# Head 7 of a two-layer trunk built from seven products for eight, like heads 2 to 6 before it

## What is computed

```python
h = rmsnorm(x, g_pre_mix)
z = h @ w_in                     # 1024 -> B | C | xin | c_q | c_kv | k_rope | gate_conv | gate_mla
yc, new_buf = short_conv(c_g * xin, conv_buf, conv_w)    # three causal taps
y_a = b_g * yc
y_b = mla_attention(q_nope, q_pe, pos, ckv_all, kpe_all, k_pos, w_uk, w_uv)    # 8 heads
merged = sigmoid(gate_conv) * y_a + sigmoid(gate_mla) * y_b
x = x + rmsnorm(merged @ w_o, g_post_mix)
x = x + rmsnorm(square(relu(rmsnorm(x, g_pre_ffn) @ w1)) @ w2, g_post_ffn)
```

## Time and profile before

| | |
|---|---|
| time of the profiled execution | 1719.35 us |
| its span in the profile | 1717.5 us |
| granted TensorE clock, mean | 0.998 |
| TensorE busy | 1704.5 us, 99%, 12735 matmuls |
| VectorE busy | 1313.3 us, 76% |
| ScalarE busy | 862.5 us, 50% |
| POOL busy | 122.3 us, 7% |
| chain that ended last | 95% TensorE, 3% VectorE, 1% DMA, 1% issue |
| weight blocks of 512 KB, issue to landing | 3.7 us median of 197 |
| sums of weights, made by POOL's DMAs | 80 of 256 KB: 7.1 us; 20 of 512 KB: 5.4; 40 of 256 KB from sums: 7.6 (medians) |

### The profile page before, as it was taken

How to read it: one execution, slowest core, us unless ns; L and a number is a source line. 1 busy time by engine, 2 the same in 40 slices (tenths; PEclk the granted TensorE clock), 3 DMA queues, 4 the chain that set the end, 5 groups by cost and what they waited for, 6 DMA issues and landing times.

```text
span 1717.5 us, 31904 instructions
## 1 busy us (share of the span) xinstructions
PE 1704.5 (99%) x12735; PEld 1690.0 (98%) x12735; DVE 1313.3 (76%) x2512; ACT 862.5 (50%) x1669; POOL 122.3 (7%) x163
## 2 busy tenths in 40 slices
PE   9999999999999999999999999999999999999997
PEld 9999999999999999999999999999999999999997
DVE  7788877767798777668688788777678887777665
ACT  7636454544554544446366364545446636444452
POOL 1412222122200000000000000000000000000000
PEclk9999999999999999999999999999999999999999
DMA  7888989898842323233133234443433313322231
GB/s 240 199 191 181 230 207 216 188 265 214 175 110 63 111 82 92 87 98 99 62 119 123 90 116 128 116 127 114 162 118 99 99 39 110 99 87 87 74 99 56
DMA packets 85619, 222.09 MB, mean 129 GB/s; under 512 B 9568, under 2 KB 21088, under 8 KB 85472
## 3 DMA queue, kind: packets, MB, share of 16 engines
q1 hardware_dynamic: 66592, 176.01, 32.1%
q0 software_dynamic: 17600, 41.95, 13.8%
q10 hardware_dynamic: 1280, 2.10, 0.4%
HBM read 209.67 MB, written 52.30 MB: 153 GB/s over the span
## 4 chain that ended last, share of the span: by engine, by line
PE 95%; DVE 3%; DMA 1%; issue 1%; ACT 0%; SPq 0%; DVEq 0%; ACTq 0%
PE ring L817 19%; PE ring L819 19%; PE ring L818 19%; PE att L817 11%; PE att L819 11%; PE att L818 11%; DMA w_raw<-blocks_in 1%; PE att L3589 1%; DVE w_lo L2092 1%; PE att L812 1%; PE att L811 1%; PE att L824 0%; PE att L3405 0%; PE att L825 0%; PE att L3744 0%
## 5 line engine op out<-in xcount | busy, mean ns | idle before, releaser
L817 PE MATMUL ring<-xs_hi,w_lo 128*128 128x288 f32 x1872 | 556.5, 297 | 1.2 <-DVE w_lo L2092 0.5
L819 PE MATMUL ring<-xs_hi,w_hi 128*128 128x288 f32 x1872 | 551.5, 295 | 0.0
L818 PE MATMUL ring<-xs_lo,w_hi 128*128 128x288 f32 x1872 | 551.3, 294 | 0.0
L2092 DVE TENSOR_TENSOR w_lo<-w_raw,w_hi 128x1024 fp32r<-128x1024 f32 (+1 forms) x364 | 370.8, 1038 | 38.7 <-ACT w_hi L1209 28.6
L817 PEld LDWEIGHTS ring<-xs_hi,w_lo 128*128 128x128 f32 x1872 | 351.6, 188 | 3.9 <-DVE w_lo L2092 1.3
L818 PEld LDWEIGHTS ring<-xs_lo,w_hi 128*128 128x128 f32 x1872 | 351.8, 188 | 1.4
L819 PEld LDWEIGHTS ring<-xs_hi,w_hi 128*128 128x128 f32 x1872 | 351.6, 188 | 0.0
L819 PE MATMUL att<-f_hi,w_hi 128*128 128x288 f32 x960 | 283.2, 295 | 0.0
L818 PE MATMUL att<-f_lo,w_hi 128*128 128x288 f32 x960 | 282.9, 295 | 0.0
L817 PE MATMUL att<-f_hi,w_lo 128*128 128x288 f32 x960 | 282.6, 294 | 0.0
L817 PEld LDWEIGHTS att<-f_hi,w_lo 128*128 128x128 f32 x960 | 180.4, 188 | 0.0
(11 more groups left out here) (346 smaller groups left out, 3189.9 us busy)
## 6 DMA issues: line engine op xcount, KB each, us to landing
w_raw<-blocks_in SPq DMA_DIRECT2D x197, 512.0 KB, 3.7
weight_sums<-blocks_in POOLq DMA_DIRECT2D x80, 256.0 KB, 7.1
w_raw<-blocks_in SPq DMA_DIRECT2D x58, 256.0 KB, 4.1
weight_sums<-blocks_in POOLq DMA_DIRECT2D x20, 512.0 KB, 5.4
weight_sums<-weight_sums POOLq DMA_DIRECT2D x40, 256.0 KB, 7.6
w_raw<-weight_sums SPq DMA_DIRECT2D x20, 512.0 KB, 4.6
w_raw<-weight_sums SPq DMA_DIRECT2D x40, 256.0 KB, 4.2
small_raw<-small_in SPq DMA_DIRECT2D x16, 320.0 KB, 4.0
```

The source lines that it names most:

```text
L817: pe.matmul(out, w[1], x[0], start=first, stop=False)
L818: pe.matmul(out, w[0], x[1], start=False, stop=False)
L819: return pe.matmul(out, w[0], x[0], start=False, stop=last)
L2092: return dve.tensor_tensor(out, a, hi.bitcast(F32), ALU.subtract)
```

## The change

- `LAST_MIXED` goes from 6 to 7: head 7 is a mixed head. There are 24 sums of weights in place of 20 (two couples per mixed head and layer), three more positions, and the extra slot takes turns with the others up to position eight (`N_EXTRA` 8).
- Head 7 has an order of its own (`MIXED_ORDER`): TensorE does product (0,0) to (0,3), projections, (0,4) to (0,6), scores, (1,0) to (1,3), turns, (1,4), (1,5), attended, block B (both halves), (1,6). The other mixed heads do block B ahead of the turns.
- VectorE: `last_mixed_head`, written out below. `small_lo(8)` moves from head 7 to behind the second `wo_out_a`, that is behind the first sample scaling; ScalarE's `small_hi(8)` to behind `wo_hi(5)`. The cache splits 0 and 1 move to behind the first four row splits. Gates with rx are plain multiplications in plain heads now (only 0 and 1 are left).
- ScalarE: rows 0 to 3 are split, then the weights of w_o 2 and 3, the copies of the new cache rows, rows 4 to 6, the second gate, row 7.
- SP: rows 0 and 1 of my are reloaded at j = 4, rows 2 to 5 (two parts) at j = 5, row 6 at j = 6, with a semaphore for rows 0 to 3 and another for the rest; cache_t and cache_pe are loaded behind the projections of head 7, cache_n and the small weights 8 at j = 6.
- Row 0 of my is kept from another place (`my[:, 5]`), and the four turned inputs lie in another order in the space of `my`.

The diff, cut (lines of context are left out):

```diff
@@ -82,7 +82,7 @@
...
-FIRST_MIXED, LAST_MIXED = 2, 6
+FIRST_MIXED, LAST_MIXED = 2, HEADS - 1
...
@@ -91,7 +91,7 @@
-N_EXTRA = 5
+N_EXTRA = 8
...
@@ -132,8 +132,8 @@
...
-        two = any(is_mixed(h) and HEAD_POS[h] + (3 if h == FIRST_MIXED else 2) <= q < HEAD_POS[h] + 7
-                  for h in range(HEADS))
+        two = any(is_mixed(h) and HEAD_POS[h] + (3 if h == FIRST_MIXED else 2) <= q
+                  < HEAD_POS[h] + (8 if h == LAST_MIXED else 7) for h in range(HEADS))
...
@@ -173,7 +173,7 @@
...
-    return pl.my[:, KC - 1, :] if k in (0, HEADS - 1) else pl.rx2[:, :]
+    return pl.my[:, 5, :] if k == 0 else pl.my[:, KC - 1, :] if k == HEADS - 1 else pl.rx2[:, :]
...
@@ -222,16 +222,17 @@
...
-FIRST_ORDER = [0, 1, 7, 8, 2, 3, 4, 5, 6]
+MIXED_ORDER = {FIRST_MIXED: [0, 1, 7, 8, 2, 3, 4, 5, 6, 9, 10, 11, 12, 13, 14, 15],
+               LAST_MIXED: [0, 1, 2, 3, 4, 5, 6, 9, 10, 11, 12, 13, 14, 7, 8, 15]}
+
+
+def mixed_part(h, n):
+
+    return MIXED_ORDER[h].index(n) if h in MIXED_ORDER else n
...
-    return HD0 + HEAD_BANKS[h] + (FIRST_ORDER.index(i) if h == FIRST_MIXED and i < 9 else i)
-
-
-def mixed_part(h, n):
-
-    return FIRST_ORDER.index(n) if h == FIRST_MIXED and n < 9 else n
+    return HD0 + HEAD_BANKS[h] + mixed_part(h, i)
...
@@ -949,12 +955,13 @@
...
-                if j in (begun, 5):
-                    sp.wait_ge(pl.sums_third, 16 * (head_sums(L, h, j // 5) + 1))
+                second = 4 if h == LAST_MIXED else 5
+                if j in (begun, second):
+                    sp.wait_ge(pl.sums_third, 16 * (head_sums(L, h, j // second) + 1))
...
-                if j in (begun, 7):
+                if j == begun or j == 7 and h != LAST_MIXED:
...
@@ -984,28 +991,34 @@
...
-                if h == HEADS - 1:
-                    sp.wait_ge(pl.my_stored, stored(L, HEADS - 2))
...
-                    if j == (4 if h == FIRST_MIXED else 3 if is_mixed(h) else 2):
+                    if h < LAST_MIXED and j == (4 if h == FIRST_MIXED else 3 if is_mixed(h) else 2):
...
-                    if h == HEADS - 1 and j == 2:
+                    if h == LAST_MIXED and j == 2:
+                        sp.wait_ge(pl.projected, L * 40 + 39)
...
-                        sp.wait_ge(pl.scored, (L + 1) * HEADS * KT)
-                        sp.dma_start(pl.naraw[:, :, :], cache_n[L]).then_inc(pl.nat_landed, 16)
...
-                        last = (1, 8, 3, 5, 9, 11, 13, 15) if h == FIRST_MIXED else (1, 3, 5, 8, 9, 11, 13, 15)
+                        last = (1, 8, 3, 5, 9, 11, 13, 15) if h == FIRST_MIXED else \
+                            (1, 3, 5, 9, 11, 13, 8, 15) if h == LAST_MIXED else (1, 3, 5, 8, 9, 11, 13, 15)
+                        if h == LAST_MIXED and j == 6:
+                            sp.wait_ge(pl.ring_full, full(L, r_mixed(h, 14)))
+                            my_load(3)
+                            sp.dma_start(pl.naraw[:, :, :], cache_n[L]).then_inc(pl.nat_landed, 16)
+                            next_small(h)
...
-                    if h == HEADS - 1:
-                        for n in ((0, 1), (2,), (3,), (), ())[j]:
-                            my_load(n)
+                    if h == LAST_MIXED and j == 4:
+                        sp.wait_ge(pl.my_stored, stored(L, HEADS - 2))
+                        my_load(0)
+                    if h == LAST_MIXED and j == 5:
+                        my_load(1)
+                        my_load(2)
...
@@ -1504,9 +1517,6 @@
...
-                if h == HEADS - 1:
-                    next_weight(-2)
-                    next_weight(-1)
...
@@ -1618,6 +1620,11 @@
...
+
+                def last_gates():
+                    eng.wait_ge(pl.ring_free, freed(L, r_mixed(h, 14)))
+                    act.activation(pl.ga[:, :], pl.ga[:, :], ACT.Tanh, scale=0.5)
+                    act.activation(pl.gb[:, cols(0)], pl.gb[:, cols(0)], ACT.Tanh, scale=0.5).then_inc(pl.gated, 1)
...
@@ -1645,6 +1652,26 @@
...
+                if h == LAST_MIXED:
+                    snapshot(0)
+                    pos_hi(L, at + 2)
+                    query_hi(h)
+                    pos_hi(L, at + 3)
+                    keys_hi(h)
+                    pos_hi(L, at + 4)
+                    pos_hi(L, at + 5)
+                    absorbed_hi(h)
+                    conv_started()
+                    snapshot(1)
+                    exponents(h)
+                    pos_hi(L, at + 6)
+                    turned_hi(h)
+                    pos_hi(L, at + 7)
+                    caches_hi()
+                    pos_hi(L, at + 8)
+                    last_gates()
+                    pos_hi(L, at + 9)
+                    return
...
@@ -1673,16 +1700,33 @@
...
-                if k < HEADS - 1:
-                    eng.wait_ge(pl.my_landed, 64 * (L + 1))
+                if k < 4:
+                    eng.wait_ge(pl.my_landed, 32 * (L + 1))
+                elif k < HEADS - 1:
+                    eng.wait_ge(pl.my_landed_rest, 32 * (L + 1))
...
-            eng.wait_ge(pl.ring_full, full(L, r_hd(HEADS - 1, 4, 0)))
-            for k in range(HEADS):
+            eng.wait_ge(pl.ring_full, full(L, r_mixed(LAST_MIXED, 7)))
+            for k in range(4):
...
+            pos_hi(L, POSITIONS + 2)
+            pos_hi(L, POSITIONS + 3)
+            eng.wait_ge(pl.latent_lo, L * 4 + 4)
+            eng.wait_ge(pl.key_lo, L * 2 + 2)
+            apart()
+            for to, src in ((pl.cth, pl.kvh), (pl.ctl, pl.kvl)):
+                act.activation(to[:, :, PAST:NT], src[:, :, NP_:NT].bitcast(F32), ACT.Copy)
+            for to, src in ((pl.kch, pl.keh), (pl.kcl, pl.kel)):
+                ins = act.activation(to[:, PAST:NT], src[:, NP_:NT].bitcast(F32), ACT.Copy)
+            ins.then_inc(pl.cache_new, 1)
+            for k in range(4, HEADS - 1):
+                x_hi_a(k)
+            eng.wait_ge(pl.ring_free, freed(L, r_mixed(LAST_MIXED, 15)))
+            act.activation(pl.gb[:, cols(1)], pl.gb[:, cols(1)], ACT.Tanh, scale=0.5).then_inc(pl.gated, 1)
+            x_hi_a(HEADS - 1)
...
@@ -1729,6 +1773,7 @@
...
+            small_hi(L, HEADS)
...
@@ -2586,20 +2629,16 @@
...
-                if h == HEADS - 1:
-                    cache_lo(1, pl.kcl[:, 0:PAST], pl.kcraw[:, 0:PAST], pl.kch[:, 0:PAST])
...
-                if h < FIRST_MIXED:
-                    own.wait()
-                    own.step(dve.tensor_tensor(pl.ga[:, :], pl.ga[:, :], pl.rx[:, :], ALU.mult))
-                if h != FIRST_MIXED - 1:
+                own.wait()
+                own.step(dve.tensor_tensor(pl.ga[:, :], pl.ga[:, :], pl.rx[:, :], ALU.mult))
+                if first:
...
-                if h < FIRST_MIXED - 1:
...
@@ -2774,8 +2812,76 @@
...
+                def last_mixed_head():
+                    upper_left(0, pl.cv[:, cols(0)])
+                    first_difference(0)
+                    second_sum(0)
+                    pos_lo(L, at + 2)
+                    query_lo(h, 0)
+                    query_lo(h, 1)
+                    pos_lo(L, at + 3)
+                    keys_lo(h)
+                    conv_state(h)
+                    lower_left(0, pl.u[:, 2:2 + NH])
+                    conv_first_half()
+                    lower_right(0, pl.v2[:, :])
+                    upper_right(0, pl.cv[:, cols(1)])
+                    conv_second_half()
+                    pos_lo(L, at + 4)
+                    pos_lo(L, at + 5)
+                    row_maxima(h)
+                    absorbed_lo(h, pl.rest)
+                    upper_left(1, pl.gb[:, cols(0)])
+                    conv_taps(h)
+                    first_difference(1)
+                    probabilities(h)
+                    second_sum(1)
+                    pos_lo(L, at + 6)
+                    turned_lo(h)
+                    lower_left(1, pl.ga[:, cols(0)])
+                    pos_lo(L, at + 7)
+                    lower_right(1, pl.ga[:, cols(1)])
+                    pos_lo(L, at + 8)
+                    src = ready(7)
+                    dve.tensor_tensor(pl.u[:, 0:NH], src, pl.cv[:, 0:NH], ALU.mult).then_inc(pl.ring_free, 1)
+                    eng.wait_ge(pl.gated, of_head(h, 2, 0))
+                    own_freed(7)
+                    own.step(dve.scalar_tensor_tensor(out=pl.ga[:, 0:NH], in0=pl.ga[:, 0:NH], scalar=1.0,
+                                                      in1=pl.u[:, 0:NH], op0=ALU.add, op1=ALU.mult))
+                    pos_lo(L, at + 9)
+                    eng.wait_ge(pl.pv_made, of_head(h, 1, 0))
+                    own.step(dve.scalar_tensor_tensor(out=my_row(pl, h)[:, 0:NH], in0=pl.gb[:, 0:NH], scalar=1.0,
+                                                      in1=pl.att[:, 1024:1024 + NH], op0=ALU.add, op1=ALU.mult))
+                    own.wait()
+                    dve.tensor_tensor(my_row(pl, h)[:, 0:NH], my_row(pl, h)[:, 0:NH], pl.ga[:, 0:NH], ALU.add)                         .then_inc(pl.merged_a, 1)
+                    for k in range(4):
```

(56 more changed lines are left out.)

85 lines of the change are left out of this document (37 added, 48 removed).

## The result

| | before | after |
|---|---|---|
| median, first comparison (6 runs each) | 1720.05 us | 1729.09 us |
| ratio, 95% interval | | 1.0053 [1.0042, 1.0064] |
| profiled execution / its span | 1719.35 / 1717.5 | 1729.10 / 1727.3 |
| matmuls | 12735 | 12687 |

What follows compares the result with a forecast made beforehand. TensorE, busy 99% of the span, was taken as the bound. Terms -6.3, -0.4, +2.0, +0.4 and +6.7 gave +2.4 us: 1721.8 for the profiled execution, 1721.4 median; 8-in-10 range 1716.0 to 1726.0.

Steps and rivals of the forecast that it cites:

- The first new wait: Head 7's turns: TensorE's transposes wait for VectorE's probabilities, 1.0 us in each layer, +2.0 in the sum.
- VectorE's backlog: From block B's first half on, VectorE has 16.85 us of work without a gap, so the first sample maximum starts late.
- The third wait: Second sample transposes: TensorE waits for VectorE's second maximum, delayed by the small split, 3.3 us per layer.
- w_o 3: Output projection block 3 waits for the split of position 11 on VectorE, 0.2 us per layer, +0.4.
- third wait's lower bound: Second sample transposes: 1.3 us if the small split and its idle time, 2.3 with the copy beside it, fall elsewhere.
- The four added sums: POOL's work lengthens into the feed-forward part, whose loads were held to have cover: 0, at most 1 us.
- The cover: Head 7's twelfth sum landed at 346.6, SP would ask at 350.4: 4 us to spare, assumed for feed-forward loads too.
- Rivals (2): Layer 0: rows 2 and 3 of my land later than 9.8 us, delaying w_o 0; 2 to 3 us more, 1724; chance 0.15.
- Rival (3): TensorE falls to the 1.2 GHz level in each long pause, slowing matmuls after it; +2.8 us, 1724.2; chance 0.10.
- t = 0: Zero of the forecast's clock: start of head 7's product (1,0), just behind its scores.
- again nowhere else: Late rows 2 and 3 of my would cost TensorE time at wo 0 only, every microsecond past 9.8 us.
- Each long pause: Assumed that TensorE falls to the 1.2 GHz level in every long pause, +2.8 us in all.

Runs made afterwards that it cites:

- third experiment: Changed kernel with the sample's small weights loaded at head 7's fourth block and split behind its turned probabilities, as before the change; 1720.08 us, 0.9999.
- sixth: Third experiment with POOL's sums dealt out anew: twelve, a pause until w_o's fifth block begins, four in layer 0, eight in layer 1; 1717.05 us, 0.9977.
- ninth: Sixth with head 7's probabilities moved ahead, taps just before block B, second-half splits dealt out later, cache splits behind w_o weight 3's split; 1713.15 us, 0.9958.
- fourth experiment: Changed kernel with both cache splits ahead of block B's first half instead of behind the four row splits; 1727.24 us, 1.0040.
- first: Changed kernel, but POOL waits with layer 1's sums until the first couple of layer 0's feed-forward part is done; 1731.63 us, 1.0061.
- fifth: Changed kernel, but POOL makes only 18 of the 24 sums during layer 0 and the last six at the head of layer 1; 1725.19 us, 1.0023.
- tenth: Kernel before, head 7 plain, with layer 1's sums held until the first couple of layer 0's feed-forward part is done; 1725.70 us, 1.0031.

## Why the prediction was wrong

**Right, and close.** The matmuls: 48 fewer at the same pace of 0.132 us, so 6.3 us. The first new wait, at the turns: 1.0 forecast, 1.04 and 1.02 measured. VectorE's backlog: the first maximum was forecast at t = 33.7 and the second at 42.9; product (1,0) starts at 1228.57, so 1262.51 and 1271.43 are t = 33.9 and 42.9. The third wait: 3.3 forecast, 2.96 and 2.94 measured. w_o 3: 0.2 forecast, 0.28 measured. Those three waits came to +9.1 in the sum and to +8.6 on the chip (2.1, 5.9 and 0.6); with them the change would have been some 2 us slower, as forecast. The third, sixth and ninth experiments confirm the mechanism by taking it away. One slip stands in the third wait's lower bound: 3.3 less the 2.3 of the small split and its idle time is 1.0, not 1.3; the third experiment, which moved just that, took 2.4 away and left 0.58 in each layer.

**Wrong, the step that failed.** "The four added sums lengthen POOL's work into the feed-forward part, whose loads have that cover too: 0, at most 1." The cover was read from SP's asking time for a sum in head 7, and stood for loads that have less of it. POOL's work ran 87 us longer, into the loads from 500 on; those issued up to 530 landed after 9.2 us in place of 4.5. That cost 2.9 us in this profile, 5 and 3 at two places in the fourth experiment's. The first, fifth and tenth experiments show it from three sides: the sums moved into the feed-forward part cost 5 us and more there in either kernel, and with the sums taken away the stall goes. The Trainium skill's page "DMA: Bandwidth & Descriptors" (section "Issuing engines are not separate DMA queues") says that DMAs issued from SP, ScalarE and GpSimd run on the same 16 engines and interleave there; the landings agree, 6.5 us beside the sums and 3.6 without them.

**Wrong, as a form.** Rivals (2) and (3) were laid out as cases that exclude each other and the forecast. Both happened, on top of it. Rival (2) with its own point: row 0's split was to begin after t = 20.4, and 393.82 is 21.75 with t = 0 at 372.07; it cost 2.3 us (2 to 3 forecast), half of it at w_o's block 2, whose low part VectorE made only behind the late row splits, which "again nowhere else" denied. The first experiment traces these rows to the same traffic of sums (11.0 us to landing with it, 4.7 without). Rival (3): +2.8 forecast, +2.9 measured. In the sum itself all three stood at nothing: the stall, the late rows and the clock behind the pauses. 1721.4 + 2.9 + 2.3 + 2.9 = 1729.5, against 1729.1. Part of that closeness is luck: 1721.4 was reckoned from a median of 1718.98, and beside the changed kernel the kernel before took 1720.05; as differences it is 10.5 us against 9.8 of the spans and 9.0 of the medians. One of the three alone would have stayed under 1726.0, any two pass it. A range for both rivals together would have reached some 1727, and only with the stall on top the time that was measured.

**"Each long pause" was too simple.** Granted clock in two stretches (columns as in the earlier trace rows), the changed kernel behind its 2.94 us wait, then the first experiment behind one of 2.95 at the same place:

```profile
1275.50:1277.00 1.50, 1.50 (x8) 1.50 (x7) 1.12 (x3) 1.39 (x4) 0.00 (x0) 0.50 0.00 0
1277.00:1279.00 2.00, 2.00 (x17) 2.00 (x16) 1.96 (x4) 0.65 (x1) 0.00 (x0) 0.99 0.00 0
```
```profile
1276.50:1278.50 2.00, 2.00 (x17) 2.00 (x18) 1.92 (x3) 1.09 (x4) 0.00 (x0) 1.00 0.00 0
```

0.50 is the 1.2 GHz level, 1.00 the 2.4 GHz level. Over the profiles of this study, and leaving out the first 12 us of each, waits of up to 2.5 us were followed by three slow matmuls at most; of thirteen from 2.66 to 5.15 us eleven were followed by some 7 to 20 of 288 columns (with the other shapes among them 1.3 to 2.8 us), and two, of 2.95 and 3.28, by two or fewer. The Trainium skill's "TensorE: Matmul & The Clock Gate" (Part 1, on the HAM clock gate) has the idle array throttled until it has been busy again; the eleven agree, the two show that a pause of that length does not always bring it about.

## What to carry to other kernels

Take work off the critical engine and the time moves to whatever stood just behind it: here 24 matmuls a layer were the cover of a VectorE queue, and one split of 1.1 us placed between two links of a chain, with its 1.15 us of idle time, cost more than the matmuls had given (4.7 us of waits and 2.9 of slow matmuls against 6.3). Before adding background DMA, ask not whether it is needed in time but which loads run beside it while it lasts, and where else it could run. And add up rivals that can happen together.
